# A last block of 64 or fewer tokens with high and low rows side by side in the experts' second product

## The reference, cut to what matters

```python
logits = (jnp.einsum('ld,de->le', h, w_router) + b_router).astype(jnp.float32)
top_val, top_idx = lax.top_k(logits, TOP_K)
gates = jax.nn.softmax(top_val, axis=-1).astype(h.dtype)
...
xs = h[tok]
hgu = lax.ragged_dot(xs, w_gate_up, group_sizes) + b_gate_up[e_sorted]
act = _clamped_swiglu(hgu)
out = lax.ragged_dot(act, w_down, group_sizes) + b_down[e_sorted]
out = out * gates.reshape(-1)[order][:, None]
return jax.ops.segment_sum(out, tok, num_segments=L)
```

## Time and profile before

| what | value |
|---|---|
| median of 3 runs | 5638.92 us (5636.2 to 5643.85) |
| the profiled execution, its own time | 5629.23 us |
| its span | 5627.8 us |
| granted TensorE clock, mean of the span | 0.978 |
| busy over the span: PE, DVE, ACT | 5336.1, 3564.8, 2642.8 us |
| matmuls of gate and up (L2577, L2579, L2583, L2584) | 9728 |
| matmuls of the second product (L2605) | 3 by 1248 |

### The profile page before, as it was taken

How to read it: one execution, slowest core, us unless ns; L and a number is a source line. 1 busy time by engine, 2 the same in 40 slices (tenths; PEclk the granted TensorE clock), 3 DMA queues, 4 the chain that set the end, 5 groups by cost and what they waited for, 6 DMA issues and landing times. The chain is left out here.

```text
span 5627.8 us, 92613 instructions
## 1 busy us (share of the span) xinstructions
PE 5336.1 (95%) x30192; PEld 4761.1 (85%) x30193; DVE 3564.8 (63%) x6831; ACT 2642.8 (47%) x5266; POOL 742.5 (13%) x595
## 2 busy tenths in 40 slices
PE   8999979789799999998989999999999999999994
PEld 7777768678699999998768999999899888888894
DVE  6667757433466667776774745655667745577776
ACT  3444321333355556666433633543546634366665
POOL 1101125332100000000130100110101100011113
PEclk9999999999899999999989999999999999999997
DMA  3332234354510111111533744644556734467677
GB/s 144 116 111 97 100 126 165 116 144 132 173 58 21 48 53 39 68 40 42 165 108 115 257 138 160 201 165 154 187 200 231 246 120 159 158 214 245 241 243 250
DMA packets 260437, 809.25 MB, mean 144 GB/s; under 512 B 22304, under 2 KB 168448, under 8 KB 224512
## 3 DMA queue, kind: packets, MB, share of 16 engines
q1 hardware_dynamic: 230352, 717.05, 36.5%
q0 software_dynamic: 27536, 84.88, 6.7%
q10 hardware_dynamic: 2336, 4.45, 0.2%
HBM read 662.84 MB, written 143.47 MB: 143 GB/s over the span
## 5 line engine op out<-in xcount | busy, mean ns | idle before, releaser
L2735 DVE TENSOR_TENSOR e_wl<-r_raw,e_wh 128x1024 fp32r<-128x1024 f32 x770 | 930.5, 1222 | 439.5 <-DVEq L2357 438.8
L2584 PE MATMUL ps<-e_hT,e_wl 128*128 128x192 f32 (+5 forms) x4096 | 1195.8, 292 | 0.0
L2651 ACT CAST e_wh<-r_raw 128x1024 fp32r (+1 forms) x770 | 790.8, 1043 | 858.5 <-ACTq L2357 828.0
L2577 PE MATMUL ps<-e_hT,e_wh 128*128 128x384 f32 (+2 forms) x2560 | 795.9, 374 | 5.0 <-PEq L2357 4.7
L2584 PEld LDWEIGHTS ps<-e_hT,e_wl 128*128 128x128 f32 x4096 | 776.0, 189 | 10.6
L2579 PE MATMUL ps<-e_hT,e_wh 128*128 128x352 f32 (+2 forms) x1536 | 528.8, 344 | 7.5 <-PEq L2357 7.5
L2583 PE MATMUL ps<-e_hT,e_wh 128*128 128x352 f32 (+2 forms) x1536 | 526.8, 343 | 0.0
L2577 PEld LDWEIGHTS ps<-e_hT,e_wh 128*128 128x128 f32 x2560 | 480.1, 188 | 49.0 <-issue 7.8
L2605 PE MATMUL ps<-e_wh,e_aTh 128*128 128x512 f32 x1248 | 504.5, 404 | 5.2 <-PEq L2357 4.9
L1791 ACT CAST a_PT<-ps 128x512 fp32r<-128x512 f32 x512 | 288.0, 589 | 464.6 <-PE ps L1731 464.6
L1746 PE MATMUL ps<-a_PT,a_V 128*128 128x256 f32 (+1 forms) x3264 | 504.3, 294 | 0.2 <-DVE a_sc L1834 0.2
(11 more groups left out here) (369 smaller groups left out, 9473.9 us busy)
## 6 DMA issues: line engine op xcount, KB each, us to landing
r_raw<-in_wgu SPq DMA_DIRECT2D x130, 2048.0 KB
r_raw<-in_wdn SPq DMA_DIRECT2D x64, 2048.0 KB
m_raw<-in_w SPq DMA_DIRECT2D x56, 1024.0 KB, 4.8
qTd<-p_qt SPq DMA_DIRECT2D x32, 640.0 KB, 6.6
e_bd<-in_bdn SPq DMA_DIRECT2D x32, 512.0 KB, 3.7
kTd<-p_kt SPq DMA_DIRECT2D x32, 448.0 KB, 4.0
a_Q<-qTd SPq DMA_DIRECT2D x7, 2048.0 KB, 9.3
a_V<-vd SPq DMA_DIRECT2D x24, 512.0 KB, 4.2
```

The costliest lines, as they stand in the source:

```text
L2577: t = pe.matmul(both, wh, E.hT[:, :, k, 0:v], start=(k == 0), stop=False)
L2584: t = pe.matmul(p[:, 0:v], wl, E.hT[:, 0, k, 0:v], start=False, stop=(k == 7))
L2651: act.copy(E.wh[:, h, x], raw[:, 2048 * h + 1024 * i:2048 * h + 1024 * i + 1024]).then_inc(E.hi_full, 1)
L2735: return dve.tensor_tensor(lo, src, hi.bitcast(F32), ALU.subtract)
```

## The change

A block b of 1, 2 or 3 is paired when the group's tokens end 64 or fewer rows into it (`PAIRED`: 192, 320 and 432 tokens; for b = 3 the limit is 432, the width that exists). Its activations then stand twice in the stationary operand: the high parts in columns 0 to 63 and the low parts in columns 64 to 127 of the block, all in `aTh`. Two products, by the high and by the low weights, give high and low rows in the two halves of a bank, and VectorE adds the halves. The width 320 joins `TAKEN`. In the widths of `PAIRED` VectorE makes the low part of the activation in two operations with a link between them, whatever the group's number of blocks. In the first block the three products come in another order; in the others four k of one product come before four of the next.

```diff
-TAKEN = (192, 256, 432, 512)
+TAKEN = (192, 256, 320, 432, 512)
 BOTH = 256
+PAIRED = {1: 192, 2: 320, 3: 432}
...
+    def later(c, h, b, rows_here):
+        g = product_bank(c, b)
+        if h == 0:
+            take(pe, E.g_free[g])
+        for k in range(4):
+            part(g, h, b, k, E.aTh, E.wh, h == k == 0, False)
+        with pe.If(rows_here > PAIRED[b]):
+            for k in range(4):
+                part(g, h, b, k, E.aTl, E.wh, False, False)
+        for k in range(4):
+            t = part(g, h, b, k, E.aTh, E.wl, False, h == 1 and k == 3)
+        if h:
+            t.then_inc(E.g_full[g], 1)
...
-            for b in range(4):
-                with present(pe, r, b):
-                    down(c, h, b, rn)
+            first(c, h, rn)
+            for b in range(1, 4):
+                with pe.If(r > b):
+                    later(c, h, b, m)
...
-                ah, al = (a[:, bass.ds(c * 2 + j, 1), 0:v].rearrange("p o n -> p (o n)") for a in (E.aTh, E.aTl))
-                low(al, y, ah).then_inc(E.aT_full, 1)
+                ah, al = (a[:, bass.ds(c * 2 + j, 1), :].rearrange("p o n -> p (o n)") for a in (E.aTh, E.aTl))
+                w = v // 128 * 128 if v in PAIRED.values() else v
+                if w < v:
+                    low(ah[:, w + 64:v + 64], y[:, w:v], ah[:, w:v]).then_inc(E.dv, 1)
+                    take(dve, E.dv)
+                low(al[:, 0:w], y[:, 0:w], ah[:, 0:w]).then_inc(E.aT_full, 1)
...
+        if b == 0:
+            scaled().then_inc(E.out_full[b], 1)
+        else:
+            with dve.If(rows_here > PAIRED[b]):
+                scaled().then_inc(E.out_full[b], 1)
+            with dve.If(rows_here <= PAIRED[b]):
+                link(scaled())
+                dve.scalar_tensor_tensor(out=E.Y[0:64, b, cols], in0=E.G[g][64:128, :], scalar=1.0 / SWIGLU_ALPHA, in1=E.Y[0:64, b, cols],
+                                         op0=ALU.mult, op1=ALU.add).then_inc(E.out_full[b], 1)
         over(E.g_free[g])
```

More of the change, by code:

```diff
@@ L2585, in gate_up, with part, first @@
                 t.then_inc(E.g_full[2 * j + z], 1)
-    def down(c, h, b, rn):
-        g = product_bank(c, b)
+    def part(g, h, b, k, x, y, start, stop):
+        return pe.matmul(E.G[g][:, :], x[:, 4 * h + k, b * 128:(b + 1) * 128], y[:, h, k * 512:(k + 1) * 512],
+                         start=start, stop=stop)
+    def first(c, h, rn):
+        b, g = 0, product_bank(c, 0)
         if h == 0:
@@ L2592, in down @@
         for k in range(4):
-            if b == 0 and k % 2 == 0:
+            if k % 2 == 0:
                 take(pe, E.w_full)
-            if b == 0 and k == 0 and c == 4:
+            if k == 0 and c == 4:
                 take(pe, E.aT_full, 2 if h else 4)
-            if b == 0 and k >= 2 and n == 1:
+            if k >= 2 and n == 1:
                 take(pe, E.aT_full)
-            if b == 0 and k == 0 and n == 0:
+            if k == 0 and n == 0:
                 bias()
-            if b == 0 and k % 2 == 1:
+            if k % 2 == 1:
                 with pe.If(rn > n):
                     rows(n, k // 2)
[L2604 to L2607, removed]
+            for m, (x, y) in enumerate(((E.aTh, E.wh), (E.aTl, E.wh), (E.aTh, E.wl))):
+                t = part(g, h, b, k, x, y, h == k == m == 0, h == 1 and k == 3 and m == 2)
+                if k == m == 0:
                     t.then_inc(E.w_free, 1)
@@ L2610, in down @@
             t.then_inc(E.g_full[g], 1)
+    def later(c, h, b, rows_here):
[11 more added lines that the diff above has]
+            t.then_inc(E.g_full[g], 1)
     ahead = Ahead(E, pe, "pe")
-    first, _, _ = ahead.group()
+    r0, _, _ = ahead.group()
     for b in range(4):
-        with present(pe, first, b):
+        with present(pe, r0, b):
             rows(b, 0)
@@ L2789, in gate_up, with outcome @@
                 take(dve, E.a_hi)
[L2790 to L2791 removed]
+                ah, al = (a[:, bass.ds(c * 2 + j, 1), :].rearrange("p o n -> p (o n)") for a in (E.aTh, E.aTl))
[4 more added lines that the diff above has]
+                low(al[:, 0:w], y[:, 0:w], ah[:, 0:w]).then_inc(E.aT_full, 1)
             dve.reg_mov(slot, now * -1 + 1)
[L2794 removed]
+    def outcome(c, b, rows_here):
         g = product_bank(c, b)
@@ L2798, in outcome, with scaled @@
             take(dve, E.out_free[b])
-        dve.scalar_tensor_tensor(out=E.Y[:, b, (c - 4) * 512:(c - 3) * 512], in0=E.G[g][:, :], scalar=1.0 / SWIGLU_ALPHA, in1=E.bd[:, (c - 4) * 512:(c - 3) * 512],
-                                 op0=ALU.mult, op1=ALU.add).then_inc(E.out_full[b], 1)
+        cols = slice((c - 4) * 512, (c - 3) * 512)
+        def scaled():
+            return dve.scalar_tensor_tensor(out=E.Y[:, b, cols], in0=E.G[g][:, :], scalar=1.0 / SWIGLU_ALPHA, in1=E.bd[:, cols],
+                                            op0=ALU.mult, op1=ALU.add)
+        if b == 0:
[7 more added lines that the diff above has]
+                                         op0=ALU.mult, op1=ALU.add).then_inc(E.out_full[b], 1)
         over(E.g_free[g])
-    was = dve.alloc_register("e_was")
+    was, was_rows = dve.alloc_register("e_was"), dve.alloc_register("e_was_rows")
     dve.reg_mov(was, 0)
+    dve.reg_mov(was_rows, 0)
     ahead = Ahead(E, dve, "dve")
@@ L2822, in experts_dve @@
     with groups(E, dve) as q:
-        left = dve.snap(was, min_val=0, max_val=4)
+        left, left_rows = dve.snap(was, min_val=0, max_val=4), dve.snap(was_rows, min_val=0, max_val=512)
         r, rn, m = ahead.group()
@@ L2826, in experts_dve @@
             with dve.If(left > b):
-                outcome(5, b)
+                outcome(5, b, left_rows)
         over(E.bd_free)
@@ L2839, in experts_dve @@
             with present(dve, r, b):
-                outcome(4, b)
+                outcome(4, b, m)
         for i in range(2):
@@ L2848, in experts_dve @@
         dve.reg_mov(was, r)
+        dve.reg_mov(was_rows, m)
         ahead.move()
-    left = dve.snap(was, min_val=0, max_val=4)
+    left, left_rows = dve.snap(was, min_val=0, max_val=4), dve.snap(was_rows, min_val=0, max_val=512)
     for b in range(4):
         with dve.If(left > b):
-            outcome(5, b)
+            outcome(5, b, left_rows)
 def norm_stage(nc, A, banks, sumd, out, eps, since, ctx):
```

## The result

The change makes the kernel slower: 5720.68 us (5718.53 to 5730.1) against 5640.31 (5636.2 to 5643.85) for the kernel before on the same chip, ratio 1.0152 (95% interval 1.0139 to 1.0164). The forecast was 5642, its range 5600 to 5672. The profiled execution took 5718.85 around a span of 5717.7, 89.9 more than before.

The account below looks back on a forecast made before the run. TensorE was taken to bound the wide groups, VectorE the 192-column gate/up phases. Minus 47.2, plus 21, 18.3, 3.9, 4.7, 0.8 and 1.1 is plus 2.6 us, 5631.8 from the profiled execution; by the median 5642, range 5600 to 5672.

Parts of the forecast that it names:

- all gate/up phases, with the next group's start: Ten 192-column gate/up phases cost 21 us; later starts of following groups add 4.7, and branches before eight others 0.8.
- second product, three one-block groups: Unpaired one-block groups gain nothing and wait for a late VectorE: 1.3 us each (bounds 0 and 2.0), 3.9 together.
- The price of a matmul and the pairs: Second product: a paired block drops 16 matmuls at 0.227 us, saving 3.63; thirteen groups save 47.2.
- six next starts: Six narrow groups following a paired one start 1.15 us later; three of 224 columns give back 0.4: 4.7 together.
- Link and split: VectorE's low part split in two with a 0.27 us link: 0.42 us a half, 0.72 where a pass ends.
- Gate/up phases: In 192-column groups TensorE follows five late VectorE halves, 2.70 us, less 0.6 of waits: 2.1 a group, 21 for ten.
- The paired narrow second products: Seven paired 192-column groups: late VectorE frees bank 1 late, losing 2.75 of 3.63 us in six, 1.8 in one: 18.3.
- The rival that came true: VectorE's longer loop code is fetched again each group, 2 us on ten narrow groups: 20, giving 5662; chance 0.1.
- Cheap links: Gate/up loop on VectorE: a half costs only 0.15 us, the pass's end stays covered, giving 5604; chance 0.17.
- room on VectorE: VectorE has slack in narrow groups after all, so nearly all 47 us saved arrive: 5592; chance 0.06.
- The lag that isn't caught up: VectorE's lag carries over into the narrow second products, all eight halves count, 83 us against 47: 5675; chance 0.16.

Follow-up runs that it names:

- after_short_moved88: Changed kernel with 320 groups paired in the 432 body (thirteen pairs, links kept), 88 semaphore steps ahead of VectorE's loop: 5639.0 us against 5633.4 for the kernel before.
- the kernel without the link: All thirteen pairs in the short loop, 88 semaphore steps ahead, no link between a 192-column half's two low parts: 5610.2 us against 5633.4 for the kernel before.
- the changed kernel moved by 28: Changed kernel with only 28 semaphore steps of VectorE put ahead of its loop: 5755.4 us against 5634.9 for the kernel before.
- the one with dead code: Kernel before with 100 never-executed instructions in VectorE's loop: 5719.1 us; with 28 semaphore steps ahead of the loop as well: 5704.8, against 5634.9 for the kernel before.

## Why the prediction was wrong, point by point

`after_short_moved88` is the change without the fetching (its 320 groups run in the body of width 432), and shows what the forecast's own steps were worth. The sums are differences to the kernel before, from first matmul to first matmul of the phases:

| step | forecast | after_short_moved88 | after |
|---|---|---|---|
| second product, six paired groups of 3 and 4 blocks | -21.8 | -21.7 | -21.7 |
| all gate/up phases, with the next group's start | +26.5 | +38.1 | +118.8 |
| second product, seven paired two-block groups | -7.1 | -15.1 | -13.2 |
| second product, three one-block groups | +3.9 | +3.3 | +4.1 |
| sum | +1.5 | +4.6 | +88.0 |

*The price of a matmul and the pairs* held: 3.60 to 3.66 us a group against 3.63. One addend of the prediction is added up wrongly: six next starts at 1.15, three of them less 0.4, make 5.7 and not 4.7, which decides nothing.

*Link and split.* From VectorE's timeline in group 28 of `after_short_moved88`, then of the kernel without the link:

```profile
5329.45 0.29 DVE L2755 TENSOR_TENSOR e_aTl<-e_up,e_aTh 128x128 f32 x1 [0.24 <-DVEq L2357]
...
5334.35 0.22 DVE L2755 TENSOR_TENSOR e_aTh<-e_up,e_aTh 128x64 f32 x1
5334.81 0.29 DVE L2755 TENSOR_TENSOR e_aTl<-e_up,e_aTh 128x128 f32 x1 [0.24 <-DVEq L2357]
...
5339.75 0.29 DVE L2755 TENSOR_TENSOR e_aTl<-e_up,e_aTh 128x128 f32 x1 [0.24 <-DVEq L2357]
```
```profile
5305.73 0.22 DVE L2755 TENSOR_TENSOR e_aTh<-e_up,e_aTh 128x64 f32 x1
5305.87 0.28 DVE L2755 TENSOR_TENSOR e_aTl<-e_up,e_aTh 128x128 f32 x1
...
5310.49 0.28 DVE L2755 TENSOR_TENSOR e_aTl<-e_up,e_aTh 128x128 f32 x1
```

The two parts start 0.46 apart, 0.24 of it idle (I took 0.27). Over the ten groups the settled halves of a pass are 4.95 and 5.33 us, against 4.55 and 4.68 before: +0.40 and +0.65 where 0.42 and 0.72 were forecast. Without the link they are 4.62 and 4.86, so the link is 0.33 and 0.47 of it. The Trainium skill's rule that a semaphore between VectorE operations costs nothing extra (VectorE: DVE Perf Modes, section The DRAIN you can't avoid) doesn't hold at this place: 0.14 us between the starts without it, 0.46 with it.

*Gate/up phases* were sized too small: 3.0 us in group 28, whose start nothing delays, against 2.1. I had TensorE follow five late halves (2.7) and gave 0.6 back for waits that a later VectorE no longer meets; seven halves at 0.40 and 0.65 are 3.6, and the measured 3.0 lies nearer to these. In group 29, which follows a paired one, it is 4.0 against 3.25. Group 0, a wide one at the stage's beginning, adds 2.1 that no step had. *The paired narrow second products* lost less than forecast: 3.63 less 1.8, not less 2.75. In group 28 TensorE stands first ahead of the transposes, then 0.44 us ahead of the second block of (5,0), where I had put a gap of 2 to 3:

```profile
5361.64 0.63 PE L2555 MATMUL ps<-ident,r_hx 128*128 128x128 f32 x4 [0.88 <-PEq L2357]
...
5369.78 1.17 PE L2589 MATMUL ps<-e_wh,e_aTh 128*128 128x512 f32 x4 [0.44 <-PEq L2357]
```

These wait for VectorE's earlier steps of the phase and its memset that frees bank 1 (5369.57 there). The late VectorE was met at an earlier wait than the one I priced, and what is waited there isn't waited again. The two errors (+11.6 and -8.0) all but cancel, so the forecast's total held by luck, for the wrong sizes: 5639.0 against 5633.4, ratio 1.0009 (1.0000 to 1.0018), where 5642 against 5639 was forecast. Without the fourth block the change would have made no difference that can be told, as forecast.

*The rival that came true* was the loop's code, and the failed step is its price and its chance: the forecast's own sum had no term for it. It named the mechanism (a longer loop fetched again in each group, VectorE standing at a branch, q14 packets in every group) and gave it 20 us and 0.1. In these runs it costs 63 to 111. Three things were mis-sized:
- The bound of 2.5 us came from the first pass, where the packets of the earlier trace rows showed and TensorE didn't stand. But group 0 has 432 columns, and there VectorE has half its time free: in the changed kernel ten of the twelve wide groups lose under 0.4 us in gate and up, though VectorE stands at the branch in them as well. A bound taken where the cost is hidden bounds nothing where it isn't. It wasn't even the same cost: at the end of that pass the kernel before has its branch at 3089.5 and its head at 3089.8, so the packets of the first pass came while VectorE ran straight on, and none of them held up the closing branch.
- I priced ten groups. The ten groups of 224 and 256 columns lose 37.9 more in gate and up, 5.8 to 7.3 each where a narrow group precedes them. Their code isn't touched; the loop's start is theirs as well.
- TensorE's clock was left out: 71.7 us at half speed, up to half of which is lost.

The chance was low because no row of the kernel before shows how near its loop is to the limit: a loop that stays leaves no trace. The compiled program does, with the packets' size: 295 instructions at 4199, a third more announced. The Trainium skill (Runtime: NRT & Kernel Launch, section Instruction fetch mechanics) states the stall at a taken branch to code that isn't held, and the traces agree, 2.7 to 6.0 us each in the changed kernel. It gives such an engine memory for 512 instructions, refilled in blocks of 256. The packets of the traces hold 128, and come one at a time. The size of 512 isn't refuted: two blocks of 256 fit every run, as said above, and so do four of 128 if one is fetched ahead of the three that a loop touches, which is my estimate from five packets a turn for four touched blocks. What the runs do refute is the reading that any loop of fewer than 512 instructions stays: 295 to 397 didn't where they lay badly.

*The other rivals.* Cheap links (5604) and room on VectorE (5592) don't hold by the halves. The lag that isn't caught up (5675) doesn't either: paired narrow second products kept 1.8 of their 3.63.

Left open: why the price of the fetching differs between places (40 more for the changed kernel moved by 28, 14 less for the one with dead code). It isn't the stand at the closing branch, which over the 31 turns is 129 us in the changed kernel and 126 in the moved one. Of the sums in the table above, that of the seven paired two-block second products goes from -13.2 to +20.6 with the move, and that of the three one-block ones from +4.1 to +14.5, while gate and up go from +118.8 to +105.3. That fits stalls that move to other branches with the block ends, but I didn't follow each.

## What to carry to other kernels

Before you price the operations that a change adds to a loop, count the instructions that each engine's loop has and where it begins: a loop of VectorE or ScalarE that reaches over one block end too many is fetched again on every turn, and code that never runs counts. The sign in a profile is an instruction queue with a steady number of packets a turn and a gap between the closing branch and the next step; a few steps ahead of the loop, or a width less in it, took it away here. Take the bound of a cost only from a place where nothing hides it.

## What the runs showed of the hardware that was not expected

- VectorE kept the code of loops of 295 to 376 instructions in nine kernels and fetched loops of 295 to 397 again in every turn in ten others; where a loop begins and ends decides. At most three blocks of 128 fits all of them, and so would at most two of 256. ScalarE's loop of 396 instructions is fetched again too. TensorE's loop has 1583 instructions in the changed kernel and q8 shows no packet between 3250 and 5550 us: so what holds for the other two doesn't hold for it.
- An instruction packet waits behind data: it starts 1.0 us after the branch on idle DMA engines and 2.5 us after it when they are 95% busy (up to 4.3 in other groups), and VectorE goes on 1.3 to 1.5 us after the packet's end.
- In group 29 of the changed kernel a stand of TensorE of 4.7 us was followed by 6.8 us at the lower clock (0.50), most of them with matmuls in a row: another engine's stall cost TensorE the wait and then more.
